# Laying the weights out in contiguous pieces, and summing the modulation along the free axis

## The reference

```python
h = rms_norm(x, norm1_g)                     # first block, once
q, ckv, qi, ki, wi, u, v, ga, gb = split(h @ w_in)
index = sum_h(relu(qi_h . ki) * wi_h)        # 8 index heads; causal, the 64 best keys of each token stay
scores = q_lat . c_kv * scale + rel_bias[bucket(distance)]      # 8 heads, softmax over the kept keys
y_a = (softmax(scores) @ c_kv) @ w_uv @ w_proj_a
y_b = (gelu(u) * (tril(w_spatial) @ layer_norm(gelu(v)) + b_spatial)) @ w_proj_b
x = x + (sigmoid(ga) * y_a + sigmoid(gb) * y_b) @ w_out
x = x + hier_moe(rms_norm(x, norm2_g))       # 32 experts of width 256, two per token, from one group of 8
for l in range(2):                           # the layers
    shift, scale, gate = split(silu(c) @ w_ada[l] + b_ada[l])   # the modulation: c is ONE vector of 1024
    h = rms_norm(x, norm_g[l]) * (1 + scale) + shift
    x = x + gate * (concat(rglru_branch(h), mlstm_branch(h)) @ w_out_2[l])
return rms_norm(x, final_g)
```

## Time and profile before

| | |
|---|---|
| median of 3 runs | 1052.12 us (1048.18 to 1054.51) |
| the profiled execution, own time | 1051.8 us |
| its span, first to last instruction | 1050.0 us |
| mean granted clock of TensorE | 0.967 |
| PE busy | 971.2 us (92%), 5569 instructions |
| DVE busy | 427.1 us (41%) |
| ACT busy | 269.8 us (26%) |
| POOL busy | 178.4 us (17%), of it 61.3 in 17 multiplications of L2151 and 40.4 in 17 additions of L2152 |
| DMA | 227.88 MB, 217 GB/s in the mean |

### The profile page before, as it was taken

One profiled execution on the slowest core, in us unless ns is written; L12 is line 12 of the kernel. 1 busy time (PEld: TensorE's weight loads), 2 busy tenths in 40 slices (PEclk: granted clock), 3 DMA queues, 4 the chain that ended last, 5 costly groups with the idle time before them and its releaser, 6 DMA issues.

```text
span 1050.0 us, 14389 instructions
## 1 busy us (share of the span) xinstructions
PE 971.2 (92%) x5569; PEld 771.1 (73%) x5569; DVE 427.1 (41%) x930; ACT 269.8 (26%) x630; POOL 178.4 (17%) x159
## 2 busy tenths in 40 slices
PE   6999799999899999776799999998999999999997
PEld 6868677788765655343288888787888888878786
DVE  1369862247622213101452454464315245265422
ACT  3231222201311211111216333234001724323301
POOL 5939997601100000000200000000000000000011
PEclk9989999989889999889899999999999999999999
DMA  9947776448989999999925444341444455423211
GB/s 290 282 156 240 226 203 198 162 150 297 422 355 419 421 420 421 422 419 421 322 79 180 133 151 160 115 126 42 153 141 128 160 160 160 149 93 120 93 48 41
DMA packets 140963, 227.88 MB, mean 217 GB/s; under 512 B 8457, under 2 KB 126562, under 8 KB 128602
## 3 DMA queue, kind: packets, MB, share of 16 engines
q1 hardware_dynamic: 136632, 221.15, 59.3%
q0 software_dynamic: 1600, 4.35, 1.6%
q10 hardware_dynamic: 2658, 1.40, 0.4%
HBM read 225.81 MB, written 1.07 MB: 216 GB/s over the span
## 4 chain that ended last, share of the span: by engine, by line
PE 77%; DVE 8%; SPq 7%; DMA 3%; issue 2%; ACT 2%; ACTq 0%; DVEq 0%
PE bank L469 25%; PE bank L1104 11%; SPq L1141 7%; PE bank L956 5%; PE bank L934 5%; PE bank L805 4%; PE bank L711 3%; PE bank L976 3%; DMA s<-in_w_up 3%; PE bank L781 2%; PE bank L841 2%; PE bank L820 2%; PE bank L452 1%; PE bank L521 1%; PE bank L991 1%
## 5 line engine op out<-in xcount | busy, mean ns | idle before, releaser
L469 PE MATMUL bank<-hT,ring 128*128 128x256 f32 x1168 | 264.0, 384 | 0.2 <-ACT s L1256 0.2
L469 PEld LDWEIGHTS bank<-hT,ring 128*128 128x128 f32 x1168 | 221.4, 192 | 35.5 <-issue 5.8
L1104 PE MATMUL bank<-ring,s 128*128 128x256 f32 x512 | 111.2, 379 | 0.0
L1104 PEld LDWEIGHTS bank<-ring,s 128*128 128x128 f32 x512 | 97.1, 190 | 13.1
L2210 POOL DMA_DIRECT2D s<-in_final_g x1 | 0.6, 604 | 475.1 <-DVE s L2053 475.1
L805 PE MATMUL bank<-s,z 128*32 128x256 f32 (+1 forms) x448 | 64.8, 434 | 8.9 <-DMA s<-in_w_up 5.7
L1828 DVE SCALAR_TENSOR_TENSOR z<-z,bank 128x256 f32<-128x256 f32 x10 | 4.2, 422 | 161.8 <-ACT z L1356 161.7
L2151 POOL TENSOR_TENSOR ring<-ring,csil 128x2048 f32<-128x2048 f32 x17 | 61.3, 3608 | 12.7 <-PE bank L495 11.7
L956 PE MATMUL bank<-ring,hT 128*128 128x256 f32 x256 | 56.6, 380 | 0.0
L934 PE MATMUL bank<-hT,ring 128*128 128x256 f32 x256 | 55.6, 379 | 0.0
L956 PEld LDWEIGHTS bank<-ring,hT 128*128 128x128 f32 x256 | 48.3, 190 | 7.7 <-issue 1.3
(11 more groups left out here) (410 smaller groups left out, 1508.5 us busy)
## 6 DMA issues: line engine op xcount, KB each, us to landing
ring<-in_w_in SPq DMA_DIRECT2D x56, 1024.0 KB, 5.5
ring<-in_w_ada SPq DMA_DIRECT2D x24, 1024.0 KB, 6.4
ring<-in_w_out SPq DMA_DIRECT2D x20, 1024.0 KB, 5.0
s<-in_w_down SPq DMA_DIRECT2D x18, 1024.0 KB, 19.9
s<-in_w_gate SPq DMA_DIRECT2D x15, 1024.0 KB, 25.6
s<-in_w_up SPq DMA_DIRECT2D x13, 1024.0 KB, 21.9
ring<-in_w_up SPq DMA_DIRECT2D x12, 1024.0 KB, 21.2
ring<-in_w_gate SPq DMA_DIRECT2D x10, 1024.0 KB, 22.3
```

The lines of the kernel that those rows point to most:

```text
L469: mm = pe.matmul(b[:, 0:T], w[:, (k0 + kb) * CW + m * P:(k0 + kb) * CW + (m + 1) * P], rhs[:, kb, :], start=(kb == 0), stop=(kb == nk - 1))
L1104: mm = pe.matmul(xo[j, tt][:, 0:CW], yT[:, kb, tt * P:(tt + 1) * P], w[:, kb, :], start=(kh == 0 and kb == 0), stop=(kh == 1 and kb == KB ...
```

## The change

What it does, by parts:

- **Layout.** `kernel()` hands the device arrays that are already rearranged (`lay_out`): all weights of the first stage and of the layers as pieces of [128, 2048] in which each partition's 8 KB are contiguous (`first_pieces`, `layer_pieces`). Every load into the ring is one transfer. The expert weights are as before.
- **x.** A transposed x (`x_T`) comes in two halves first; the sum of squares runs over partitions by eight matmuls with a matrix of ones (L446), ACT takes the root, DVE the reciprocal and the eight products of hT. x itself is loaded behind the sixth piece. 12 matmuls on constants stand ahead (`WARM_START`).
- **Vectors** come as columns; nothing is turned on PE. wi is part of the latent piece. The gate weights of the mLSTM and their biases are one transfer each.
- **Bias and masks.** The relative bias is a table by distance and head (`bias`), which DVE adds to the mask (`sc = bias + maskb`) before it adds the scores. The causal mask is a constant `tri` added in the first index step. w_spatial comes transposed, and b_spatial is broadcast and added by DVE (`gsum`).
- **Modulation.** The pieces of w_ada are laid with the output column on the partition and the 1024 inputs along the free axis. POOL multiplies the piece by `csb` (c's silu times two, in every partition), and two activations of ACT with an accumulated sum write `adac`; for the last seven pieces two instructions of DVE do both. PE has no part in it. `ADA_LAG` is 1.
- **Expert pieces.** Three of the twelve fixed expert pieces are issued early, between pieces 14, 18 and 22 of the first stage (`EARLY_LOADS`), and the buffers of `moe_slots` stand in another order.

The diff, cut to its core:

```diff
-A_TURN = 3
+A_TURN = 0
+WARM_START = 12
-ADA_LAG = 2
+ADA_LAG = 1
+EARLY_LOADS = {14: 1, 18: 1, 22: 1}
...
 # PE, ada_job
-                if n >= ADA_LAG:
-                    n -= ADA_LAG
-                    pe.wait_ge(*ada_done(n))
-                    b = A.acquire(pe, f"ada{n}")
-                    for m in range(2):
-                        mm = pe.matmul(b[:, m:m + 1], adasum[:, n % 3, m * P:(m + 1) * P], allone[:, 0:1],
-                                       start=True, stop=True)
-                    mm.then_inc(A.done, 1)
...
+            for _ in range(WARM_START):
+                pe.matmul(psum[0][:, 0:P], allone[:, :], allone[:, :], start=True, stop=True)
+            b = B.acquire(pe, "ssq")
+            for kb in range(KB):
+                pe.wait_ge(S["sq_v" if kb // 2 % 2 else "sq_a"], 2 * (kb // 4) + kb % 2 + 1)
+                mm = pe.matmul(b[:, 0:T], allone[:, :], sqT[:, kb, :], start=(kb == 0), stop=(kb == KB - 1))
...
-            projT(w, 1, hT, A, "kiT")
+            for kb in range(KB):
+                for o in (0, 64):
+                    mm = pe.matmul(b[o:o + 64, 0:T], wv[:, kb, 0:64], hT[:, kb, :], start=(kb == 0), stop=(kb == KB - 1))
...
-                        pe.matmul(b[:, 0:ns], anti[:, :], biasT[:, h, T - ns:T], start=True, stop=False)
                         pe.matmul(b[:, 0:ns], qT[o:o + 64, h // 2, tt * P:(tt + 1) * P], kvT[o:o + 64, h // 2, 0:ns],
...
 # SP
+                sp.dma_start(slots_of[i][:, :], src).then_inc(slot_full[i], 16)
...
+                for _ in range(EARLY_LOADS.get(n, 0)):
+                    load_expert(len(early))
...
 # ACT, ada_job
-                if n >= 0:
+                if 0 <= n < ADA_POOL:
                     l, j = divmod(n, 3 * D // CW)
-                    out_copy(adac[:, l, 2 * j:2 * j + 2], 2)
+                    w = ring[ada_chunks[n] % RING]
+                    act.wait_ge(S["ada_scaled"], n + 1)
+                    step(f(w[:, 0:D], w[:, 0:D], ACT.Copy, scale=0.5, accum_out=adac[:, l, 2 * j:2 * j + 1]))
+                    step(f(w[:, D:2 * D], w[:, D:2 * D], ACT.Copy, scale=0.5, accum_out=adac[:, l, 2 * j + 1:2 * j + 2]),
+                         S["ada_summed"])
...
 # DVE, start, heads, gm, last seven pieces
+            step(v.reciprocal(rbc, rbc))
+            for kb in range(KB):
+                step(stt(hT[:, kb, :], xT[:, kb, :], colA[:, kb:kb + 1], rbc, ALU.mult, ALU.mult), S["hT_ready"])
...
+                    step(tten(sc[:, tt, 0:ns], bias[:, h, T - ns:T], maskb[:, tt, 0:ns], ALU.add))
+                    b = B.take(v)
+                    step(stt(sc[:, tt, 0:ns], b[:, 0:ns], SCALE, sc[:, tt, 0:ns], ALU.mult, ALU.add), B.free)
...
+                step(tten(gsum, b[:, 0:T].rearrange("p (c t) -> p c t", c=TT),
+                          bsp[:, g, :].unsqueeze(1).broadcast_to([P, TT, P]), ALU.add))
...
+                    step(stt(w[:, 0:D], w[:, 0:D], 0.5, csb, ALU.mult, ALU.mult, accum_out=adac[:, l, 2 * j:2 * j + 1]))
...
 # POOL, ada_sums
-                    step(g.tensor_tensor(w, w, csil[:, :].unsqueeze(2).broadcast_to([P, KB, CW]), ALU.mult))
-                    step(g.tensor_tensor(w[:, 0:4, :], w[:, 0:4, :], w[:, 4:8, :], ALU.add))
-                    step(g.tensor_tensor(w[:, 0:2, :], w[:, 0:2, :], w[:, 2:4, :], ALU.add))
-                    step(g.tensor_tensor(adasum[:, n % 3, :], w[:, 0, :], w[:, 1, :], ALU.add), S["ada_summed"])
+                    step(g.tensor_tensor(w, w, csb.unsqueeze(1).broadcast_to([P, 2, D]), ALU.mult), S["ada_scaled"])
...
 # kernel(): the piece of w_ada
+    elif kind == "ada":
+        l, j = at
+        t = w["w_ada_2"][l][:, j * CW:(j + 1) * CW].T.reshape(2, P, D).transpose(1, 0, 2)
```

More of the change, by code:

```diff
@@ L566, in _ @@
             assert not idx_left
-            pe.wait_ge(S["rowsL_loaded"], 16 * 20)
-            for l in range(LAYERS):
-                b = B.acquire(pe, f"colL{l}")
-                tr(b[:, 0:P], rowsL[:, l, :])
-                tr(b[:, P:P + 16], rowsM[:, l, :], 16).then_inc(B.done, 1)
-            pe.wait_ge(S["rel_loaded"], 32)
-            b = B.acquire(pe, "relrow")
-            pe.matmul(b[0:HEADS, :], relw, reltab, start=True, stop=True).then_inc(B.done, 1)
-            pe.wait_ge(S["const_ready"], 1)
             pe.wait_ge(S["ckv_ready"], 1)
@@ L724, in _ @@
             route(3, (1,), (C.free, C.upto("xT31")))
-            for _ in range(ADA_LAG):
-                ada_job()
+            assert state["ada"] == ADA_CHUNKS
             pe.wait_ge(S["routed"], 1)
@@ L1193, in roots @@
                 step(f(view, view, ACT.Sqrt), S["root_ready"])
-            def sumsq(ready=((), ()), junk=squares):
-                for tt in range(TT):
-                    if ready[tt]:
-                        act.wait_ge(*ready[tt])
-                    step(f(junk[:, tt, :], x[:, tt, :], ACT.Square, accum_out=small[:, tt:tt + 1]), S["ssq_ready"])
             def load_root_table():
@@ L1240, in _ @@
                 step(f(ckv[:, tt, :], b[:, 0:RANK], ACT.Copy))
[L1241 to L1243 removed]
+                step(f(pT[:, 0, tt, :], b[:, 0:RANK], ACT.Square, accum_out=small[:, 4 + tt:5 + tt]))
+                step(f(wi[:, tt, :], b[:, RANK:RANK + 8], ACT.Copy, scale=IDX_SCALE), A.free)
             roots(small[:, 6:8])
@@ L1594, in _ @@
                              S["relu_used"])
-            for l in range(LAYERS):
-                b = B.take(v)
-                step(v.tensor_copy(colL[:, l, :], b[:, 0:P]))
-                step(v.tensor_copy(colM[:, l, :], b[:, P:P + 16]), B.free)
+            v.wait_ge(S["rowsL_loaded"], 32)
             step(tsc(lneg, colL[:, :, V_LAM:V_LAM + KB], -1.0, None, ALU.mult))
@@ L1604, in _ @@
             b = B.take(v)
-            step(v.tensor_copy(relrow, b[0:HEADS, :]), B.free)
-            b = B.take(v)
             step(tsc(cT, b[:, 0:T], colA[:, 16:17], None, ALU.mult), B.free)
```

484 lines of the change are left out of this document (203 added, 281 removed).

## The result

The changed kernel took 1065.1 us in the median of 4 runs (1062.25 to 1068.79) against 1051.34 (1048.18 to 1054.51, 4 runs): a ratio of 1.0129, with an interval of 1.01 to 1.0158. It is slower by 13.8 us, where 2.6 us less was forecast; it also lies above the range.

A forecast was written before the change was run, and what follows sets the result against it. The prediction took the moment the expert order is known (292.1 us) as the bound, with byte-bound expert loads behind it. Gains 9.0 and 6.35 less a loss of 12.8 gave 2.6 us: 1049.2 us, range 1042 to 1056 (8 in 10: 1033 to 1061).

The forecast's parts named there:

- the start: Transposed x in two halves: column sums to 7.2, first projection at 10.0 for 15.28; gain 4.7 us, 3 at low clock.
- from there to K: Index phase up to the keys: its end at 64 to 68, taken as 66 for 68.3; gain 2.3 us (0 to 4.4).
- u and v: Pure PE work: four adasum pairs (1.5 us) and the turn of w_spatial (0.5) go; gates start at 99.3 for 103.6.
- norm and head 0: Layer norm to the first output matmul: 119 to 123, taken as 120.5 for 129.51; gain so far 9.0 us.
- the heads: Head loop: period 13.9 us for 11.42, in all 85.4 us for 72.55; loss 12.8 us.
- behind the heads: After the last head's output: bias matmuls -3.2, output projections -1.5, w_out -1.65; gain 6.35 us.
- the end of POOL's third product in the index phase: POOL runs three products without a gap from about 24, so DVE's small step ahead of the root may wait to 37.3.
- one wait for POOL in the norm: Layer norm: six DVE steps take some 4 us free, up to 4 us more if one meets POOL.
- the 1.3 us taken for clock and POOL in a head: Clock falls up to 1.7 us, POOL's delay 0 to 1.8, overlapping: period between 12.6 and 15.5, taken as 13.9.
- The slower rival: Half clock and POOL in every head, before its output matmul: 3 us a head, period 15.5, total 1058.9; chance 0.22.
- the stage behind the order: Expert stage and layers, from the known order to the end: 757.9 us as before.
- Bytes that nobody waits for: First-stage ring loads and early expert loads: contiguous pieces shorten DMA no PE stall ends in, and early loads don't count.

The follow-up runs named there:

- e7: e6 with the second ring piece held until x landed, c loaded behind ACT's squares, 8 more constant matmuls before the projection: 1015.74 us, ratio 0.9637.
- e2: Changed kernel with POOL's product over a w_ada piece cut to 2x16 columns for 2x1024, ACT's sums at full length: 1047.01 us, ratio 0.9949.
- e1: Changed kernel with ACT's two sums in the head loop moved behind the copies of pT and the head's output: 1036.72 us, ratio 0.9866.
- e4: Changed kernel with 12 constant 128x128 matmuls filling PE's gap before the wait for the probabilities' copy in every head: 1061.35 us, ratio 1.0083.
- e6: Changed kernel with all 24 modulation pieces summed by DVE in its idle time, none on POOL or ACT: 1016.16 us, ratio 0.9649.
- e5: Changed kernel with the edits of e2 and e4 together, short POOL product and filled PE gap: 1035.57 us, ratio 0.9839.
- e8: Kernel before the change with only the ring pieces laid out contiguously, one transfer each: 1052.28 us, ratio 0.9992.
- e12: e7 with the sum behind head 0's softmax moved behind head 1's, 8 warm matmuls for 12, and no early expert loads: 1010.53 us, ratio 0.9602.
- e3: Changed kernel with ACT's two sums run over 16 columns each for 1024, in their places, POOL's product at full length: 1049.0 us, ratio 0.9954.

## Why the prediction was wrong

Between the forecast and the trace lie 20.1 us at the known order (15.9 us between the forecast and the median, of which this execution is 3.7 above). By the positions of the table they are: the start 3.7, from there to K 3.7, u and v 0.9, norm and head 0 5.7, the heads 7.3, and behind the heads 1.2 better. Three steps of the prediction failed: the end of POOL's third product in the index phase, one wait for POOL in the norm where there were two, and the 1.3 us taken for clock and POOL in a head.

**The start, 3.7 us late.** I let the second half of x land at 5.2 and the column sums trail to 7.2. The halves took 5.3 us in the median, and the squares of the second half began at 7.8. PE's eight sums took 0.51 us each, and the warm matmuls were in their way:

```profile
1.23 5.49 PE L442 MATMUL bank<-allone 128*128 128x128 f32 x24 [1.23 <-POOL allone L1968]
6.51 4.05 PE L446 MATMUL bank<-z,allone 128*128 128x256 f32 x16
```

16 records of 128x256 in 4.05 us are 0.25 us a record, for 0.22 later. When e7 had the second half's squares begun at 6.5, the sums still ended at 10.0, because the 12 warm matmuls lasted to 6.6; with 8 they ended at 9.3. The projection itself took 15.76 us for 13.98, at a granted clock of 0.55 from 14 to 16 us: I had named that risk (a gain of 3 us for 4.7) and left it out of the sum. By itself none of this is a loss at K, as the forecast had PE 8 us early there: in e2 the projection was as late (13.58, 15.82 us long), and with the product short K came at 62.2, 3.8 us ahead of the forecast. What the late start did is to bring DVE's next step into POOL's way.

**The index phase, K 7.4 us late.** The mechanism was named (POOL covers the small DVE step ahead of the root) and its end taken at 37.3, from three products without a gap since 24. It was 42.4. DVE and POOL, with rows of the norm behind them:

```profile
38.05 4.36 DVE L1431 TENSOR_SCALAR small<-small 128x2 f32<-128x2 f32 x1 [19.61 <-ACT s L1143]
...
112.66 3.40 DVE L1507 TENSOR_SCALAR s<-s,small 128x512 f32<-128x512 f32 x1
...
118.86 4.89 DVE L1510 TENSOR_TENSOR s<-s,gateB 128x512 f32<-128x512 f32 x1
```

```profile
37.87 4.51 POOL L2035 TENSOR_TENSOR ring<-ring,rxp 128x2048 f32<-128x2048 f32 x1 [2.33 <-DMA ring<-in_first_pieces]
...
118.69 4.51 POOL L2035 TENSOR_TENSOR ring<-ring,rxp 128x2048 f32<-128x2048 f32 x1 [2.92 <-DMA ring<-in_first_pieces]
```

The products began at 26.4, and the third waited 2.33 us for its piece, since the DMA was full to 40 us (a share of 0.99 from 30 to 40 us in the window above, 0.28 in the next 10), and then covered DVE's 0.17 us step for 4.36 us. It is a race: in e1, whose program is the same to this point, DVE's step came at 36.53, ahead of the product at 37.48, took 0.17, and K was at 67.7. In e4 it was 69.3. What moved it was the projection, which started 0.4 us earlier in e1 and took 14.6 us for 15.8. So the trace of one execution carries some 4 to 6 us of chance here. Even e1's 67.7 is later than the 66 of the forecast.

**Norm and head 0, 5.7 us.** I allowed one meeting with POOL, up to 4 us, and 120.5 left room for 1.6 of it. There were two, the rows at 112.66 and 118.86: 2.85 and 4.2 us over the free 0.55 and 0.69 (free in e6, where the six steps take 4.0 us in all). The 0.83 that I had read as free was not: in e6 that step takes 0.55. With the product short, head 0 came at 115.8; in e6, with neither POOL nor ACT in the way, at 112.5.

**The heads, 7.3 us.** ACT's part came as worked out: PE's gap 3.1 us, and 12.44 us a period when only that is left (e5), for 12.5 to 12.6. What failed is the price of the two things on top. I took 1.3 us for clock and POOL together, because they overlap; over the 12.44 the trace has 1.7 in the three periods of 14.1 and 14.2, 2.6 and 2.9 in two others, and 5.3 in the first, where DVE's add took 3.88 us beside a product. DVE, then POOL:

```profile
142.75 0.29 DVE L1523 TENSOR_REDUCE rt<-s 128x1 f32<-128x128 f32 x1
143.07 3.88 DVE L1520 TENSOR_TENSOR s<-s 128x256 f32<-128x256 f32 x1
```

```profile
142.16 4.51 POOL L2035 TENSOR_TENSOR ring<-ring,rxp 128x2048 f32<-128x2048 f32 x1 [3.04 <-DMA ring<-in_first_pieces]
```

That the two overlap was right and went further than I saw: each alone holds the period of the middle heads at 14.1 (e2, e4), where my sum had 13.9 for both. The mean of six periods is 15.07. The slower rival had this mechanism with a period of 15.5; it came nearest, but as a sum of two prices where each alone gives 14.1, and its total of 1058.9 was too low because index phase and norm went wrong for it too.

**Behind the heads** the gain was 7.7 us for 6.35, and **the stage behind the order** did not move, as forecast. Bytes that nobody waits for gave nothing (e8, e12), as forecast. So the frame of the argument held (the sums stand in PE's waits, and the order sets the end), and the error is in the prices of waits for POOL, three times in one direction: in the way to K, in the 5.7 us and in a part of the 7.3. In each I counted a wait for POOL once or in part where it came more often or lasted longer. In the heads this is no accident: each product starts when a piece lands, and the piece lands when ACT, which waits for DVE, has freed its buffer (the circle of e4). That the same holds in the index phase and the norm was not shown.

On the two places of the Trainium skill: the product took 4.515 us on average (17 of them, 76.8 us), which agrees with the 4497 ns of the Trainium skill (GPSIMD Engine Reference, 3.1 Elementwise). The rule of the Trainium skill (TensorE: Matmul & The Clock Gate, Why this matters for your kernels), that idle stretches between bursts bring the array back to half rate, agrees with the changed kernel's heads and with e4, where the filled gap left it at 1.00; e6 has a gap of 2.95 us and e3 one of 3.37 us that were followed by full rate.

## What to carry to other kernels

A reduction moved to an idle engine can cost much more than its length if it is issued ahead of what others wait for on that engine: with the same two activations ahead of a copy the heads took 92.7 us, behind it 66.3, with the period of a kernel in which ACT has no such work at all (10.08 us in e1 and e6). Where a step that another engine's instruction holds up stands in a loop, look for the circle (buffer freed, load, product, step, job) and add it up; it can be as long as the wait that you see, and hide behind it. Taking away one of two bounds of the same height then shows nothing (e4), so try them together (e5). And try the engine that has the operation in one instruction, in its gaps: DVE's multiply with an accumulated sum did 24 pieces in 2.5 us each and made room on two other engines.

## What the runs showed of the hardware

- Some DVE steps wait for a POOL product of 4.5 us beside which they begin, and end with it or up to 0.6 us behind: TENSOR_TENSOR (3.88 and 4.89 us for 0.42 and 0.69) and TENSOR_SCALAR (4.36 and 3.40 us for 0.17 and 0.55) with operands from SBUF. With the product in four instructions a small step takes 1.04 to 1.31 us. Other steps beside a product were not held: one that reads a bank (L1522 at 142.43, 0.29 us), TENSOR_REDUCE (142.75, 0.29), RECIPROCAL (112.45, 0.17), and in e3 the MAX8 and MATCH_REPLACE8 of the selection (0.29 and 0.28 from 75.2 to 76.6 beside the product at 74.81).
- 12 matmuls in a gap of 3.1 us kept the granted clock at 1.00 in every window from 130 to 210 us; without them it was 0.66 in 150 to 160 us.
- In the first 6 us matmuls of 128x128 took 0.23 us a record (24 in 5.49 us) though the window rows give a granted clock of 1.00; in the filled heads they took 0.12 (24 in 2.84 us).
- A fourfold drop in packets (140963 to 35492) for the same bytes changed no time in this kernel.
